# Rounding and splitting whole weight chunks instead of halves in a three-block network kernel

## The reference

```python
logits = h @ router_w; top_val, top_idx = top_k(logits, 2); gates = softmax(top_val)
y = gate * ((silu(x @ w1[e]) * (x @ w3[e])) @ w2[e])    # 8 experts, 1024 -> 2816 -> 1024
```

## Time and profile before

| | before |
|---|---|
| Median of 3 runs | 1804.99 us (1804.19 to 1805.96) |
| Profiled execution | 1805.39 us |
| Its span in the profile | 1803.0 us |
| Granted TensorE clock, mean | 0.999 |
| PE busy | 1776.5 us (99%) |
| DVE busy | 1386.2 us (77%) |
| ACT busy | 1199.0 us (66%) |
| HBM read | 452.62 MB, 261 GB/s over the span |

### The profile page before, as it was taken

How to read it: one execution, slowest core, us unless ns; L and a number is a source line. 1 busy time by engine, 2 the same in 40 slices (tenths; PEclk the granted TensorE clock), 3 DMA queues, 4 the chain that set the end, 5 groups by cost and what they waited for, 6 DMA issues and landing times.

```text
span 1803.0 us, 31572 instructions
## 1 busy us (share of the span) xinstructions
PE 1776.5 (99%) x10841; PEld 1548.8 (86%) x10841; DVE 1386.2 (77%) x1977; ACT 1199.0 (66%) x1874; POOL 80.9 (4%) x135
## 2 busy tenths in 40 slices
PE   8999999999999999999999999999999999999998
PEld 7989899899999987888887888888788898889997
DVE  5674777855566788998989898998999877875555
ACT  6556565544456577877877787877877766674444
POOL 2000000000020010000000000000000022300000
PEclk9999999999999999999999999999999999999999
DMA  8546343565569479999999999999999743246552
GB/s 302 190 142 222 129 152 130 173 203 179 184 229 338 161 270 372 384 379 360 392 363 372 358 387 362 368 371 358 406 379 354 266 169 111 78 144 199 183 186 95
DMA packets 133648, 468.70 MB, mean 260 GB/s; under 512 B 15678, under 2 KB 20702, under 8 KB 133296
## 3 DMA queue, kind: packets, MB, share of 16 engines
q1 hardware_dynamic: 120664, 437.18, 66.7%
q0 software_dynamic: 5360, 19.41, 2.8%
q10 hardware_dynamic: 7528, 10.80, 1.9%
HBM read 452.62 MB, written 17.85 MB: 261 GB/s over the span
## 4 chain that ended last, share of the span: by engine, by line
PE 82%; DVE 9%; DMA 4%; ACT 3%; issue 1%; ACTq 0%; SPq 0%; DVEq 0%
PE ps L282 23%; PE ps L283 23%; PE ps L284 23%; DVE low L267 4%; DMA ring<-in_stream 4%; PE ps L295 1%; PE ps L289 1%; ACT high L258 1%; PE ps L290 1%; PE ps L1167 1%; PE ps L435 1%; PE ps L1202 1%; PE ps L3115 1%; PE ps L1060 1%; PE ps L1179 1%
## 5 line engine op out<-in xcount | busy, mean ns | idle before, releaser
L267 DVE TENSOR_TENSOR low<-ring,high 128x1024 fp32r<-128x1024 f32 x828 | 981.0, 1222 | 201.7 <-ACT high L258 198.7
L258 ACT CAST high<-ring 128x1024 fp32r<-128x1024 f32 x828 | 839.4, 1050 | 206.1 <-PE ps L284 145.0
L282 PE MATMUL ps<-high,xT_high 128*128 128x256 f32 (+1 forms) x1632 | 564.7, 346 | 2.0 <-DVE h L1553 1.0
L283 PE MATMUL ps<-low,xT_high 128*128 128x256 f32 (+1 forms) x1632 | 550.2, 337 | 0.0
L284 PE MATMUL ps<-high,xT_low 128*128 128x256 f32 (+1 forms) x1632 | 547.7, 336 | 0.0
L282 PEld LDWEIGHTS ps<-high,xT_high 128*128 128x128 f32 x1632 | 307.0, 188 | 38.9 <-issue 4.5
L284 PEld LDWEIGHTS ps<-high,xT_low 128*128 128x128 f32 x1632 | 306.9, 188 | 36.2
L283 PEld LDWEIGHTS ps<-low,xT_high 128*128 128x128 f32 x1632 | 307.7, 189 | 30.2
L282 PE MATMUL ps<-high,smallT_high 128*128 128x512 f32 (+2 forms) x578 | 224.1, 388 | 1.2 <-DVE smallT_low L3341 1.2
L283 PE MATMUL ps<-low,smallT_high 128*128 128x512 f32 (+2 forms) x578 | 224.1, 388 | 0.0
L284 PE MATMUL ps<-high,smallT_low 128*128 128x512 f32 (+2 forms) x578 | 223.2, 386 | 0.0
(11 more groups left out here) (430 smaller groups left out, 1623.2 us busy)
## 6 DMA issues: line engine op xcount, KB each, us to landing
ring<-in_stream SPq DMA_DIRECT2D x828, 512.0 KB, 5.2
slot_rows<-mix POOLq DMA_DIRECT2D x16, 512.0 KB, 10.8
mix<-slot_rows POOLq DMA_DIRECT2D x7, 512.0 KB, 7.3
bias_rows<-bias_line ACTq DMA_DIRECT2D x2, 1536.0 KB, 12.5
expert_rows<-proj POOLq DMA_DIRECT2D x6, 512.0 KB, 7.1
wide<-in_wide_rows ACTq DMA_DIRECT2D x5, 512.0 KB, 5.7
work<-bias_rows ACTq DMA_DIRECT2D x2, 1024.0 KB, 8.8
h<-in_x SPq DMA_DIRECT2D x2, 512.0 KB, 5.6
```

Source lines behind the costliest of these rows:

```text
L258: A.e.copy(k.high[:, slot, cols], k.ring[:, slot, cols]).then_inc(flow.high_made, 1)
L267: V.e.tensor_tensor(k.low[:, slot, cols], k.ring[:, slot, cols], k.high[:, slot, cols].bitcast(F32), ALU.subtract).then_inc(flow.split, 1)
L282: T.e.matmul(out, x[0], w[0], start=start, stop=False, **more)
L283: T.e.matmul(out, x[0], w[1], start=False, stop=False, **more)
```

## The change

Where a helper is called for both halves, ACT waits for both landings and casts 2048 columns by one instruction, raising `high_made` by 2; DVE waits for that and subtracts 2048 columns by one instruction, raising `split` by 2. Calls for one half are as they were, and so are the loads by halves and all other waits.

```diff
 def split_high(A, k, flow, c, i=0, halves=(0, 1)):
 
     slot = c % RING
+    if halves == (0, 1):
+        for half in halves:
+            A.e.wait_ge(flow.landed[slot][half], i * 16 + (c // RING + 1) * 16)
+        if type(i) is not int or c >= RING:
+            A.e.wait_ge(flow.used, i * RING + (c + 1 - RING))
+        A.e.copy(k.high[:, slot, :], k.ring[:, slot, :]).then_inc(flow.high_made, 2)
+        return
     for half in halves:
...
 def split_low(V, k, flow, c, i=0, halves=(0, 1)):
 
     slot = c % RING
+    if halves == (0, 1):
+        V.e.wait_ge(flow.high_made, i * (2 * RING) + (2 * c + 2))
+        V.e.tensor_tensor(k.low[:, slot, :], k.ring[:, slot, :], k.high[:, slot, :].bitcast(F32),
+                          ALU.subtract).then_inc(flow.split, 2)
+        return
     for half in halves:
```

## The result

| | before | changed |
|---|---|---|
| Median | 1805.28 us (1804.19 to 1805.96, 4 runs) | 1938.99 us (1935.16 to 1945.99, 4 runs) |
| Ratio | | 1.0743 (1.0727 to 1.0759) |
| Profiled execution / span | 1805.39 / 1803.0 us | 1935.78 / 1933.8 us |
| Mean granted clock | 0.999 | 0.995 |

The forecast was 1916 us, 1845 to 1985. On the page of the changed kernel PE is busy 1818 us of 1934, and the chain that ended last has changed hands: PE was 82% of it and is 43%; load, cast and subtraction of weights were some 9% and are 43% together.

What follows compares the result with a forecast made beforehand. The prediction took PE to bound the kernel, by a small margin in the experts, where the ring's loop would now bind. Its terms 98+8+3+2 = +111 us on the profiled 1805.4 gave 1916 us, range 1845 to 1985.

Steps and rivals of the forecast that it cites:

- What bounds: Whole kernel: PE's own work sets the time nearly everywhere, by a small margin in the experts.
- The half microsecond: Experts, before the change: a half's own loop of 2.45 us plus a 5.5 us flight left some half a microsecond.
- the circle: Experts: a ring slot's issue, flight, cast, subtraction without PE; 4.94 us + flight against 8.625 a round, 88 times: +98 us.
- The flight of 4.8: Experts: time from a transfer's issue to its landing, taken as 4.8 us; 4.2 would give +45, 5.5 +160.
- POOL's transfers: 13 transfers of 512 KB, some 1.3 us each, no longer hidden by a margin: up to 17 us, half taken, +8.
- The start: PE's first product waits for all of chunk 0 and begins at 14.37 us instead of 11.31: +3 us.
- Elsewhere: Feed-forwards and projections: mostly hidden by PE; six casts on a path straight to PE, 0.84 us each, less some 3: +2.
- a late split: A chunk's whole cast and subtraction end 4.27 us after the cast's release instead of 3.43: 0.84 us later.
- That PE stays the bound: Rival, experts: the second half lands within 3.7 us of its issue, the loop fits in 8.625; 1809 us, chance 0.05.
- That DVE was the true limit: Rival, experts: DVE's relief of 0.07 us for 264 chunks, 18 us, makes it faster; 1790 us, chance 0.03.
- A crowded queue: Rival, experts: all slots load at once, flights of 7.4 us, loop 12.3, +326 us; 2140 us, chance 0.04.

Runs made afterwards that it cites:

- the short second half: The changed kernel, but the second transfer of each of the experts' 264 chunks loads 256 of its 1024 columns: 1837.4 us, ratio 1.0181.
- the longer cast: The changed kernel, but in the experts each whole cast is 8 casts of 256 columns in a row: 1982.0 us, ratio 1.0984.
- the kernel with the experts by halves: The changed kernel, but casts and subtractions in the experts go by halves as before, whole everywhere else: 1817.3 us, ratio 1.0068.
- the kernel with the late chunks by halves: The changed kernel, but by halves in the experts, the dense feed-forwards' loops and 17 chunks whose whole cast stood in the chain: 1805.7 us, ratio 0.9999.
- the start by halves: The changed kernel, but casts and subtractions of the experts and of chunk 0 go by halves: 1814.2 us, ratio 1.0045.

## Why the prediction was right, and where its sizes were off

- **What bounds** was read rightly: PE, with a small margin in the experts. The half microsecond that the prediction gave this margin was not measured. The change turned the circle into the bound, as the short second half shows, and the longer cast in part.
- **The circle** had 4.94 us + flight. Its own part measured 5.30: 0.78 for SP where I had put 0.65, 0.21 from landing to cast where a single wait had taken 0.02, 0.10 for 0.03 to the subtraction; cast and subtraction were right (1.91 for 1.95, 2.29). The flight of 4.8 measured 4.7 to 4.8. The small steps were 0.36 us too short, 32 us in 88 rounds. Against that, PE's round was read as 8.625 us where it is 8.72, because the 759 us hold 87 steps from product to product and not 88; this made the term 9 us too large. The term was +98, and +8 for POOL's transfers, which the measured rounds contain and which no run takes apart. The stage is 115.6 us longer. That the sum of the two came so near has some luck in it.
- **That the flight can be taken as a fixed term** is the weak step of the method: with the second issue 0.6 us earlier it was about as much longer. In the kernels with full transfers the last landing came 5.4 to 6.1 us after the last release (means over their chains between 700 and 1400 us), but only 4.1 us with the longer cast.
- **The start** was put at +3 and is worth 2 to 3: the first product was forecast for 14.37 us and stands at 14.57, but not all of that reaches the end.
- **Elsewhere** was +2 and is some +9 (the 12 us of the kernel with the experts by halves, less the start). This is the term that was furthest off in proportion. The price of a late split, 0.84 us, was about right (0.87 in the one shown above), their number not: six were counted and some ten were paid (9 us at 0.84, an estimate), of the 16 found in the chain. I counted casts that were in the chain already, and a longer split also brings others into it. In the changed kernel a dip of PE's clock adds to it (last section).
- **Rivals.** That PE stays the bound needed a flight of 3.7; with the kernel's own second flights of 4.7 it is refuted. That DVE was the true limit is refuted: DVE was relieved and the experts took longer, and outside them the relief brought nothing (1806.8 and 1805.7 us). A crowded queue did not come: the rate fell to 324 GB/s and the median flight to 4.1 us. The Trainium skill's advice in Perfetto Trace Analysis, section Optimizing Scalar/DVE Operations, to break instructions up where these engines are not saturated but hold others up, fits here: merging them cost 116 us in the experts. Its advice to group where an engine is saturated did not apply, though DVE was 91% busy in that stage, since PE was busier.

## What to carry to other kernels

Splitting a step in pieces can pay when the step is part of a buffer's circle (load, use, release), even on an engine with time to spare: add up the circle and compare it with the time in which the consumer uses all the slots. Count that time from one use to the same use a round later, not as a stretch divided by the number of rounds. Merging saved 0.07 us for each pair of subtractions and 0.09 for each pair of casts here, and delayed the split by some 0.8 us. It cost nothing clear of the noise only where a chunk is used for far longer than the circle takes and nothing waits behind the merged instruction, and even there it gained nothing. Do not take the flight of a queued transfer as fixed: measure from release to last landing, and expect it to move when the rest of the circle does.

## What had not been expected

An earlier issue brought next to nothing: after a release by halves or whole, with one transfer or two, the last landing came after about the same time. Less data loaded shortened it, and so it was in the kernel with the longer cast, where the round was longest. Why is open.

PE's granted clock fell to its lower level, 1.2 GHz, for most of 10 us (0.53 in the mean), while the router's products ran, with PE busy all of the time and no idle time ahead of it. First the kernel before, then the changed one, at about the same work:

```profile
640.00:650.00 10.00, 10.00 (x89) 9.95 (x90) 6.12 (x38) 8.27 (x18) 1.18 (x2) 1.00 0.10 30
```

```profile
650.00:660.00 10.00, 10.00 (x51) 10.00 (x51) 4.67 (x31) 5.25 (x7) 1.45 (x2) 0.53 0.10 33
```

It shows in 9 of the 12 profiles, also in that of the kernel with the late chunks by halves, which loses nothing, and not in those of before, of the experts by halves or of the start by halves; in the changed kernel the same three groups of products (4.05, 3.61 and 4.50 us in its chain, 3.03, 1.89 and 3.69 before) took 3.6 us longer. The kernel with whole splits in the experts alone has this dip too, is as before up to there, and reaches the experts' first product 3.6 us late (660.2 for 656.6), which fits. It is 3 to 4 us of the changed kernel's 134, and no part of the experts' 116. Apart from the last microseconds of every kernel, further dips of about 5 us to 0.66 or so come only in the experts of kernels in which PE idles there. How much these cost was not measured. They may be why the changed kernel's four runs spread over 11 us where those of before spread over 2: the longest run has the lowest mean clock (0.987, against 0.992 to 0.995). What sets the dips off stays open.
